# Leaving the residual unscaled: gate and bias divided by alpha, the first residual tiles made in the last merge chunk

## The chip, the cores and the metric

One NeuronCore of a Trainium2 chip runs the whole layer. Its engines are TensorE (PE, and PEld for its weight loads), VectorE (DVE), ScalarE (ACT), GpSimd (POOL) and SyncE (SP); SP and POOL issue nearly all transfers here. The metric is the device time of one execution, in microseconds (us). Engines wait for one another by semaphores written out by hand.

## The reference

One layer of a decoder trunk on `x` of 2048 tokens by 1024 channels, all in float32:

```
h    = x * (1 + scale(c)) + shift(c)
proj = h W_in + b_in                       # q k v | z_attn | u g_b g_c z_conv | two merge gates
y_A  = (dilated attention * silu(z_attn)) W_pA
y_B  = (g_b * conv3(g_c * u) * silu(z_conv)) W_pB
m    = sigmoid(g_A) * y_A + sigmoid(g_B) * y_B
out  = LayerNorm(alpha * x + gate(c) * (m W_out + b_out)) * ln_g + ln_b     # alpha = 2 ** 0.25, eps = 1e-5
```

The mean and variance of the layer norm are taken over the 1024 channels of each token. Where the argument of the norm is divided by alpha, its standard deviation is divided by alpha too; so the same output comes from `x + (gate/alpha) * (m W_out + b_out)`, if the variance is multiplied by alpha squared ahead of eps and the centred value by alpha.

## The kernel before

All products are done in fp32r with each operand split into a high and a low part, in three passes (L1224 high by high, L1229 high by low, L1232 low by high). Big projections are done by a seven-product scheme (`NP = 7`): per group of 2 x 2 blocks, sums and differences of weight blocks are multiplied by sums and differences of activation blocks, and a group's seven results (p0 to p6) are added into four outputs. A product is four matmuls of 128x128 by 128x512 in each of three passes. ScalarE rounds the high parts (`round_w`, `round_t`, `round_to`), VectorE forms the low parts by subtraction (`split_w`, `split_t`, `split_to`) and the sums of weights (`combine`).

The stages, in order: the input projection (`NS` products in all; in it attention, convolution and gates are worked in between; its gate stage forms the `gate` row and multiplies `w_out` by it, one 128-row slice k at a time, `load_wo_raw`, `scale_wo`, `store_wos`); the merge, `NMU = 32` units of 4 token chunks by 8 channel tiles (`project_att`, `project_conv` on TensorE, `gate_att`, `merge` on VectorE, `store_m` on POOL); and the output projection with the norm, 8 groups of seven products, each group two tiles of 128 tokens. `M0 = 24` is the first unit of the last merge chunk. The merged activations take the place of weights in the output projection, and `w_out`'s blocks and their combinations, to(0) to to(6), that of activations; `load_to(p)` on SP waits for the convolution products that last read the places it fills, to(4), to(5) and to(6) for all of them.

The residual. `xs` is a ring of six places for tiles of `x`, 128 tokens by 1024. `load_x(h)` (L907) on SP loads the two tiles of a group, `scale_x` (L1614) on ScalarE multiplies them by alpha, `residual(tt)` (L1159) on POOL adds the row `gb_d` = gate * b_out to all 128 partitions by an accumulating transfer, and `take_y` on VectorE adds the projection's results from PSUM. `take_y(NS)`, the first one, waits for both tiles of its group (`r_in`); it signals `p1_out`, which the third product of the group, p2, waits for, since p0, p2, p4 and p6 of a group share one PSUM bank (`bank`). In the same way p4 waits for `take_y` of p2, and p6 for that of p4.

After that `deviation` (L1606, L1609) on ScalarE and `center` (L2138, L2141) on VectorE finish a tile and `shift_row` (L1163) on POOL stores it. `finish_last` does the last one.

The row gate * b_out is made in the last merge chunk: SP loads `b_out` and `ada_d` (the gate row, stored earlier) as broadcasts (L965, L966), VectorE multiplies them at M0+1 and waits for them there, POOL stores one row to `gb_d` (L1169). The order on each engine is the order of the code: in the last chunk each engine runs its work unit by unit, and in the output projection VectorE's step m takes product m-1, then `center`, `combine`, `split_w(m + 3)` and in the first three steps `split_to`. The stores of the last chunk go to places which the gate loads of units three later reuse (`m_last`); SP issues these loads (L837) in turn with `load_to` (L894).

Of the kernel before, what the change touches and what calls it, by code (L numbers as in the profile page):

```python
# [8 lines left out]
ALU = mybir.AluOpType  # L9
# [190 lines left out]
def build(nc, x, x_t, c, w_ada_t, w_gate, b_ada, cols_h, w_first, w_tiles, w_pa, w_pc, w_out, b_out, ln_g, ln_b, out):  # L200
# [20 lines left out]
    mix_d = dram("mix_d", (KT, P, SEQ))  # L221
    ada_d = dram("ada_d", (1, D))

    with ExitStack() as top:
# [126 lines left out]

        gb = view(3584, D)
        g_bc = view(5632, D)
        b_bc = view(6656, D)
        squares = view(8704, D)
        xs = (view(4608, D), part[:].rearrange("p a n -> p (a n)")[:, 0:D], view(0, D), view(1024, D), view(2048, D), view(7680, D))
        wq = view(3584, 4, CH)
# [106 lines left out]
        gbc_done = sem("gbc_done")  # L464
        ada_out = sem("ada_out")
        wos_ready = sem("wos_ready")
# [32 lines left out]
        gb_ready = sem("gb_ready")  # L499
        x_scaled = sem("x_scaled")  # L500
        r_in = [sem(f"r_in{r}") for r in range(2)]
# [153 lines left out]
        with nc.Block() as block:  # L655
            @block.sync
            def _(sp):
# [48 lines left out]
                def load_t(ph, p):  # L706
                    if p == 0:
                        if ph == 1:
                            for idx in (0, 2, 3):
                                sp.wait_ge(hk_out[idx], 16 * KH)  # L710
                            sp.wait_ge(tk_out, 16 * 4 * KH)
                        if ph == 2:
                            for n in ("b11", "b21", "b22", "t1", "t2", "t3", "rest"):
                                sp.wait_ge(dumped[n], 16)
                            sp.wait_ge(ada_out, 16)
                            sp.wait_ge(za_out, 64)
                            for r in range(2):
                                sp.wait_ge(wos_out[r], 16 * 4)
                    if p >= STAGED:
                        sp.wait_ge(prod, FIRST[ph] - NP + p + 1)  # L720
                    if p >= 4:
                        sp.wait_ge(t_hi_done, NP * ph + T_MORE + p - 3)
                    dst = t_stage[ph][p] if p < STAGED else t_raw[:, p]
                    sp.dma_start(dst, tr_d[(0, 1, 0)[ph], p]).then_inc(t_in[p % 4], 16)
# [39 lines left out]
                def load_wo_raw(k):  # L764
                    sp.wait_ge(gbc_done, 2)
                    if k >= 2:
                        sp.wait_ge(wos_out[k % 2], 16 * (k // 2))
                    sp.dma_start(gate_w[:, k % 2], w_out2[:, k, :]).then_inc(gw_in[k % 2], 16)
# [127 lines left out]
                def load_x(h):  # L896
                    if h == 0:
                        sp.wait_ge(gb_ready, 1)
                    if h in (1, 2):
                        wait_m_last()  # L900
                        sp.wait_ge(ya_done, NMU)
                    if h >= 2:
                        sp.wait_ge(x_scaled, 2 * h - 2)
                    if h >= 3:
                        sp.wait_ge(outs[h % 3], 32 * (h // 3))
                    for tt in (2 * h, 2 * h + 1):
                        sp.dma_start(xs[tt % NX], x2[tt * P:(tt + 1) * P, :]).then_inc(x_in[h % 2], 16)  # L907
# [40 lines left out]
                for n in range(NMU):  # L948
# [10 lines left out]
                    if n == M0:  # L959
                        load_m(0)  # L960
                        load_m(1)
                        load_to(0)
                        sp.wait_ge(ya_done, M0)
                        sp.wait_ge(ada_out, 16)
                        sp.dma_start(gb, b_out.broadcast_to([P, D])).then_inc(bc_in, 16)  # L965
                        sp.dma_start(xs[0], ada_d.broadcast_to([P, D])).then_inc(bc_in, 16)  # L966
                    for p, when in ((1, 3), (2, 4), (3, 6)):
                        if n == M0 + when:
                            load_to(p)
                    if n == M0 + 5:  # L970
                        load_x(0)
                load_to(4)
                load_to(5)
                load_to(6)
                sp.wait_ge(gb_ready, 1)
                sp.wait_ge(ya_done, NMU)
# [17 lines left out]
            def _(pool):  # L994
# [121 lines left out]
                for m in range(NPAIRED, NS + 2):  # L1116
# [21 lines left out]
                    if m - 2 in TWO_AT[1:]:  # L1138
                        store_att(TWO_AT.index(m - 2) - 1)
                    if m == BG2 + 26:  # L1140
                        pool.wait_ge(gbc_done, 2)
                        pool.dma_start(ada_d, gate_bc[0:1, :]).then_inc(ada_out, 16)
                    for k in range(KT):
# [11 lines left out]
                def residual(tt):  # L1155
                    pool.wait_ge(x_scaled, tt + 1)
                    if tt >= 4:
# [7 lines left out]
                for n in range(NMU):  # L1165
                    store_m(n)
                    if n == M0 + 1:
                        pool.wait_ge(gb_ready, 1)
                        pool.dma_start(gb_d, gb[0:1, :]).then_inc(gb_out, 16)  # L1169
                        pool.wait_ge(gb_out, 16)  # L1170
                residual(0)
                residual(1)
                for h in range(NO):
# [242 lines left out]
            def _(act):  # L1416
# [182 lines left out]
                def deviation(tt):  # L1599
                    r = tt % 2  # L1600
                    if tt == LAST:
                        act.wait_ge(var_ready, 1)
                        nc.scalar.activation(std[:, r:r + 1], mv[:, 1:2], ACT.Sqrt, bias=eps[:, 0:1]).then_inc(std_ready, 1)
                        return
# [4 lines left out]
                    nc.scalar.activation(std[:, r:r + 1], ssq[:, r:r + 1], ACT.Sqrt, bias=eps[:, 0:1],  # L1609
                                         scale=1.0 / D).then_inc(std_ready, 1)  # L1610

                def scale_x(tt):
                    act.wait_ge(x_in[tt // 2 % 2], 32 * (tt // 4 + 1))
                    nc.scalar.activation(xs[tt % NX], xs[tt % NX], ACT.Identity, bias=0.0, scale=ALPHA).then_inc(x_scaled, 1)  # L1614

# [70 lines left out]
                for n in range(NMU):  # L1686
# [9 lines left out]
                    for q, when in enumerate((2, 3, 5, 7)):  # L1696
                        if n == M0 + when:
                            round_w(NS + q)
                    if n == M0 + 7:
                        scale_x(0)  # L1700
                        scale_x(1)

                for m in range(NS, NALL + 2):
                    if m + 4 < NALL:
                        round_w(m + 4)
                    if m < NS + 3:
                        round_to(m - NS + 4)
                    h, p = (m - NS) // NP, (m - NS) % NP
                    if p == 3 and h < NO - 1:
                        scale_x(2 * h + 2)  # L1710
                        scale_x(2 * h + 3)
                    if p == 6:
# [5 lines left out]
            def _(dve):  # L1718
# [277 lines left out]
                def scale_wo(k):  # L1996
                    dve.wait_ge(gbc_done, 2)
                    dve.wait_ge(gw_in[k % 2], 16 * ((5, 4)[k % 2] + k // 2 + 1))
                    tt_op(gate_w[:, k % 2], gate_w[:, k % 2], gate_bc, ALU.mult).then_inc(wos_ready, 1)

# [127 lines left out]
                def center(tt):  # L2128
# [5 lines left out]
                    if tt < 2:  # L2134
                        dve.wait_ge(bc_in, 64)
                    dve.wait_ge(nmu_ready, tt + 1)
# [131 lines left out]
                for n in range(NMU):  # L2268
# [10 lines left out]
                    if M0 + 1 <= n <= M0 + 3:  # L2279
                        combine(NG, n - M0 - 1)  # L2280
                    if n == M0 + 1:
                        dve.wait_ge(bc_in, 32)
                        tt_op(gb, gb, xs[0], ALU.mult).then_inc(gb_ready, 1)
                    for p, when in enumerate((2, 5, 6, 7)):
# [66 lines left out]
```

## Time and profile before

| | us |
|---|---|
| median of 3 runs | 1878.07 (1877.03 to 1879.09) |
| the profiled execution | 1877.03 |
| its span in the trace | 1875.2 |
| TensorE busy | 1831.5 (98%) |
| VectorE busy | 1241.3 (66%) |
| ScalarE busy | 876.3 (47%) |
| GpSimd busy | 201.6 (11%) |

The profiled execution is one of the three runs; its span is 1.8 us shorter than its time. In the timeline a row is: start, duration, engine, line, operation, written tile and read tiles, shapes, count, and in brackets the idle time of the engine ahead of it with what ended it. A row of windows is: the stretch; its length, then for each engine (PE, PEld, DVE, ACT, POOL) busy time and count of instructions; then the granted TensorE clock (1.00 is full), the share in which the 16 DMA engines moved data, and GB/s. `room` is the large scratch area in SBUF; many tiles lie in it, some of the `xs` among them; `part` is another such place. A row for SPq or POOL with DMA_DIRECT2D is the issue of a transfer.

### The profile page before, as it was taken

The numbers are of one execution on the slowest core, as the hardware profiler recorded it, in microseconds if no ns is written. First come the engines' busy times: TensorE is split into PE (matmuls) and PEld (weight loads), VectorE is DVE, ScalarE is ACT, GpSimd is POOL, SyncE is SP. The second block draws the span as 40 slices with busy tenths as digits, with TensorE's granted clock in tenths as the row PEclk, the third lists the DMA queues.
The fourth block names the chain that finished last, engine by engine and source line by source line (L and its number), as shares of the span: only waits on it lengthen the run. The fifth ranks groups of instructions, "written<-read, shape, count | busy, mean of one in ns | idle before, by whom it ended". The sixth has DMA issues, their size and how long they took to land.

```text
span 1875.2 us, 24771 instructions
## 1 busy us (share of the span) xinstructions
PE 1831.5 (98%) x8783; PEld 1490.9 (80%) x8783; DVE 1241.3 (66%) x2185; ACT 876.3 (47%) x1567; POOL 201.6 (11%) x327
## 2 busy tenths in 40 slices
PE   8999999999999999999999999999999999996997
PEld 7788888888888888877878888888888888885875
DVE  8755744456666666665686666666577665646886
ACT  5544633445555555666665445545444400014442
POOL 0223011100000000111110000000111000001110
PEclk9999999999999999999999999999999999998998
DMA  9866523332222222555762222232583987777782
GB/s 371 297 231 242 201 108 112 104 120 85 97 97 85 85 95 82 177 178 194 275 225 93 79 90 80 85 107 85 177 291 120 346 219 198 234 255 220 211 227 86
DMA packets 162234, 312.32 MB, mean 167 GB/s; under 512 B 35808, under 2 KB 87776, under 8 KB 157888
## 3 DMA queue, kind: packets, MB, share of 16 engines
q1 hardware_dynamic: 133072, 209.68, 34.5%
q0 software_dynamic: 28752, 100.46, 15.8%
q8 instruction: 71, 1.16, 0.3%
q10 hardware_dynamic: 288, 0.59, 0.1%
q14 instruction: 51, 0.42, 0.1%
HBM read 218.10 MB, written 92.58 MB: 166 GB/s over the span
## 4 chain that ended last, share of the span: by engine, by line
PE 86%; DVE 5%; DMA 4%; issue 2%; ACT 1%; SPq 1%; POOL 0%; DVEq 0%; ACTq 0%
PE acc L1224 23%; PE acc L1229 23%; PE acc L1232 23%; PE acc L1378 2%; PE acc L1386 2%; PE acc L1382 2%; PE score L1289 2%; PE xb L1322 2%; DVE room L1725 1%; DVE t_lo L1725 1%; PE acc L1240 1%; PE xb L1305 1%; PE pt_o L1305 1%; DMA part<-gb_d 1%; DMA vt_d<-room 1%
## 5 line engine op out<-in xcount | busy, mean ns | idle before, releaser
L1224 PE MATMUL acc<-t_hi,w_hi 128*128 128x512 f32 x1888 | 519.7, 397 | 5.5 <-DVE room L1725 4.4
L1229 PE MATMUL acc<-t_lo,w_hi 128*128 128x512 f32 x1888 | 505.8, 390 | 0.0
L1232 PE MATMUL acc<-t_hi,w_lo 128*128 128x512 f32 x1888 | 505.4, 389 | 0.0
L1229 PEld LDWEIGHTS acc<-t_lo,w_hi 128*128 128x128 f32 x1888 | 354.4, 188 | 75.8
L1232 PEld LDWEIGHTS acc<-t_hi,w_lo 128*128 128x128 f32 x1888 | 354.4, 188 | 74.9
L1224 PEld LDWEIGHTS acc<-t_hi,w_hi 128*128 128x128 f32 x1888 | 344.5, 188 | 86.7 <-issue 13.7
L1725 DVE TENSOR_TENSOR room<-acc,part 128x512 f32<-128x512 f32 x198 | 136.7, 690 | 216.6 <-PE acc L1232 214.8
L1505 ACT ACTIVATE part<-acc,cols 128x512 f32<-128x512 f32 x198 | 136.5, 689 | 209.3 <-PE acc L1232 208.9
L1725 DVE TENSOR_TENSOR w_lo<-w_raw,w_hi 128x512 fp32r<-128x512 f32 x278 | 187.4, 686 | 38.7 <-ACT w_hi L1488 37.1
L1488 ACT CAST w_hi<-w_raw 128x512 fp32r<-128x512 f32 x270 | 166.2, 616 | 99.0 <-PE acc L1232 96.7
L1488 ACT CAST w_hi<-s_tmp 128x512 fp32r<-128x512 f32 x203 | 125.6, 619 | 177.9 <-PE acc L1232 146.7
L1725 DVE TENSOR_TENSOR room<-room 128x512 f32<-128x512 f32 (+3 forms) x217 | 156.3, 724 | 62.7 <-ACT room L1535 30.6
L1725 DVE TENSOR_TENSOR w_lo<-s_tmp,w_hi 128x512 fp32r<-128x512 f32 x203 | 139.4, 687 | 64.7 <-ACT w_hi L1488 62.3
L1570 ACT ACTIVATE room<-room 128x128 f32<-128x128 f32 (+1 forms) x192 | 86.4, 451 | 54.8 <-DVE room L1971 54.6
L1076 POOL DMA_DIRECT2D att_d<-room x48 | 34.5, 718 | 529.9 <-DVE room L1978 529.9
L1725 DVE TENSOR_TENSOR w_raw<-w_raw 128x512 f32<-128x512 f32 x98 | 67.4, 688 | 5.0 <-DVE room L1725 0.5
L1967 DVE CUSTOM_DVE_ANT_0 room<-score,room 128x128 f32<-128x128 f32 (+1 forms) x192 | 58.7, 362 | 17.1 <-PE score L1289 16.8
L1725 DVE TENSOR_TENSOR s_tmp<-w_raw,s_tmp 128x512 f32<-128x512 f32 x74 | 51.0, 690 | 27.5 <-PE acc L1232 24.4
L1725 DVE TENSOR_TENSOR t_lo<-t_raw,t_hi 128x2048 fp32r<-128x2048 f32 (+1 forms) x29 | 57.6, 1992 | 14.4 <-ACT t_hi L1597 10.7
L1589 ACT CAST t_hi<-t_raw 128x2048 fp32r<-128x2048 f32 x6 | 11.4, 1907 | 113.5 <-DMA t_raw<-conv_d 113.5
L1098 POOL DMA_DIRECT2D gate_d<-room x64 | 34.9, 547 | 243.2 <-ACT room L1521 243.1
L1224 PE MATMUL acc<-t_hi 128*128 128x512 f32 x152 | 42.1, 399 | 17.7 <-DVE room L1725 17.7
(257 smaller groups left out, 2102.1 us busy)
## 6 DMA issues: line engine op xcount, KB each, us to landing
w_raw<-in_w_tiles SPq DMA_DIRECT2D x132, 512.0 KB, 4.4
gate_d<-room POOLq DMA_DIRECT2D x64, 256.0 KB, 3.9
qk_d<-room POOLq DMA_DIRECT2D x24, 512.0 KB, 5.1
w_raw<-gate_d SPq DMA_DIRECT2D x24, 512.0 KB, 6.2
room<-qk_d SPq DMA_DIRECT2D x74, 128.0 KB, 3.1
t_raw<-tr_d SPq DMA_DIRECT2D x8, 1024.0 KB, 7.2
conv_d<-room POOLq DMA_DIRECT2D x16, 512.0 KB, 3.0
w_raw<-mix_d SPq DMA_DIRECT2D x16, 512.0 KB, 7.3
```

The source lines that it names most:

```text
L1224: nc.tensor.matmul(to, hi_w[:, k], hi_t[:, k], start=(first and k == 0), stop=False, skip_group_check=True)
L1229: nc.tensor.matmul(to, hi_w[:, k], lo_t[:, k], start=False, stop=False, skip_group_check=True)
L1232: mm = nc.tensor.matmul(to, lo_w[:, k], hi_t[:, k], start=False, stop=(last and k == KH - 1), skip_group_check=True)
L1289: mm = nc.tensor.matmul(sc_ps[:, h, columns(j, s)], q_two[rows_h, s], keys, start=True, stop=True)
L1305: tr = nc.tensor.transpose((po, xb)[s][:, (2 * h + half) * P:(2 * h + half + 1) * P], prob[:, h, (2 * s + half) * P:(2 * s + half + 1) * P ...
L1322: mm = nc.tensor.matmul(o_ps[cols_h, s * P:(s + 1) * P], v_two[:, s + half, cols_h], prob_t[:, s, (2 * h + half) * P:(2 * h + half + 1) * ...
L1378: nc.tensor.matmul(to, w_h[:, k], b_half(True, k), start=(k == 0), stop=False)
L1488: nc.scalar.copy(w_slot(hi_parts, n), src).then_inc(hi_done, 1)
L1505: ins = nc.scalar.activation(to, src, ACT.Identity, bias=col(gr.tb if p == 1 else gr.ta))
L1570: ex = nc.scalar.activation(prob[:, h, o], prob[:, h, o], ACT.Exp, bias=all_m[:, t, h, b], scale=SCALE, accum_out=all_d[:, t, h, b])
L1725: return nc.vector.tensor_tensor(o, a, b, op)
L1967: own_t.up(nc.vector.tensor_tensor_reduce(out=prob[:, h, o], in0=sc_ps[:, h, o], in1=bm[:, h, o.start - 2 * P * s:2 * P], scale=1.0, scala ...
```

## The change

- `x` is no longer scaled. `scale_wo` multiplies `w_out` by gate and by 1/alpha, the bias row is gate * b_out / alpha, `deviation` uses alpha squared, and `g_bc` (ln_g on all partitions) is multiplied by alpha once, on ScalarE in step NS+4.
- The bias row is formed in the gate stage, on one partition, just ahead of the first `scale_wo`, and POOL stores it to `gb_d` there. `ada_d` and the two broadcasts in the last merge chunk are gone.
- `load_x(0)` goes from unit M0+5 to M0+2; `residual(0)` and `residual(1)` go from behind the merge loop to behind `store_m(M0 + 3)` in POOL's queue.
- The ring of `xs` has other places, so that `load_x(1)` and `load_x(2)` no longer wait for the last merge stores.
- `residual(tt)` waits for the load of `x` itself.

```diff
-        xs = (view(4608, D), part[...][:, 0:D], view(0, D), view(1024, D), view(2048, D), view(7680, D))
+        xs = (part[...][:, 0:D], view(4608, D), view(3584, D), view(7680, D), view(9728, D), view(10752, D))
@@ SP
                 def load_wo_raw(k):
                     sp.wait_ge(gbc_done, 2)
+                    if k == 0:
+                        sp.dma_start(gate_acc[0:1], b_out).then_inc(b_row_in, 16)
...
                 def load_x(h):
                     if h == 0:
-                        sp.wait_ge(gb_ready, 1)
+                        sp.wait_ge(ya_done, M0)
                     if h in (1, 2):
-                        wait_m_last()
                         sp.wait_ge(ya_done, NMU)
                     if h >= 2:
-                        sp.wait_ge(x_scaled, 2 * h - 2)
+                        sp.wait_ge(r_in[h % 2], 32 * (h // 2))
...
                     if n == M0:
                         load_m(0)
                         load_m(1)
                         load_to(0)
-                        sp.wait_ge(ya_done, M0)
-                        sp.wait_ge(ada_out, 16)
-                        sp.dma_start(gb, b_out.broadcast_to([P, D])).then_inc(bc_in, 16)
-                        sp.dma_start(xs[0], ada_d.broadcast_to([P, D])).then_inc(bc_in, 16)
...
-                    if n == M0 + 5:
+                    if n == M0 + 2:
                         load_x(0)
...
-                sp.wait_ge(gb_ready, 1)
@@ POOL
-                    if m == BG2 + 26:
-                        pool.wait_ge(gbc_done, 2)
-                        pool.dma_start(ada_d, gate_bc[0:1, :]).then_inc(ada_out, 16)
+                    if m == BG2 + 29:
+                        pool.wait_ge(gb_ready, 1)
+                        pool.dma_start(gb_d, gate_acc[0:1]).then_inc(gb_out, 16)
...
                 def residual(tt):
-                    pool.wait_ge(x_scaled, tt + 1)
+                    pool.wait_ge(x_in[tt // 2 % 2], 32 * (tt // 4 + 1))
...
                 for n in range(NMU):
                     store_m(n)
-                    if n == M0 + 1:
-                        pool.wait_ge(gb_ready, 1)
-                        pool.dma_start(gb_d, gb[0:1, :]).then_inc(gb_out, 16)
+                    if n == M0 + 3:
                         pool.wait_ge(gb_out, 16)
-                residual(0)
-                residual(1)
+                        residual(0)
+                        residual(1)
@@ ScalarE
-                def scale_x(tt):
-                    act.wait_ge(x_in[tt // 2 % 2], 32 * (tt // 4 + 1))
-                    nc.scalar.activation(xs[tt % NX], xs[tt % NX], ACT.Identity, bias=0.0, scale=ALPHA).then_inc(x_scaled, 1)
...
+                    if m == NS + 4:
+                        act.wait_ge(bc_in, 32)
+                        nc.scalar.activation(g_bc, g_bc, ACT.Identity, bias=0.0, scale=ALPHA).then_inc(g_scaled, 1)
...
-                    if p == 3 and h < NO - 1:
-                        scale_x(2 * h + 2)
-                        scale_x(2 * h + 3)
@@ VectorE
                 def scale_wo(k):
                     dve.wait_ge(gbc_done, 2)
+                    if k == 0:
+                        dve.wait_ge(b_row_in, 16)
+                        nc.vector.scalar_tensor_tensor(out=gate_acc[0:1], in0=gate_acc[0:1], scalar=1.0 / ALPHA, in1=gate_bc[0:1],
+                                                       op0=ALU.mult, op1=ALU.mult).then_inc(gb_ready, 1)
                     dve.wait_ge(gw_in[k % 2], 16 * ((5, 4)[k % 2] + k // 2 + 1))
-                    tt_op(gate_w[:, k % 2], gate_w[:, k % 2], gate_bc, ALU.mult).then_inc(wos_ready, 1)
+                    nc.vector.scalar_tensor_tensor(out=gate_w[:, k % 2], in0=gate_w[:, k % 2], scalar=1.0 / ALPHA, in1=gate_bc,
+                                                   op0=ALU.mult, op1=ALU.mult).then_inc(wos_ready, 1)
...
-                    if n == M0 + 1:
-                        dve.wait_ge(bc_in, 32)
-                        tt_op(gb, gb, xs[0], ALU.mult).then_inc(gb_ready, 1)
```

## Rows read from the trace of the kernel before

**Rows 1.** The page's head: the span and its instructions.

```profile
span 1875.2 us, 24771 instructions
```

**Rows 2.** TensorE's waits over the span: total, times, longest.

```profile
PE acc L1224 <- DVE room L1725: 22.0, 12, 15.9
```

**Rows 3.** Windows over the start of the output projection.

```profile
1686.20:1691.80 5.60, 5.60 (x25) 4.32 (x23) 3.86 (x4) 5.20 (x6) 0.00 (x0) 1.00 0.85 292
1691.80:1707.70 15.90, 0.01 (x1) 0.00 (x0) 2.43 (x6) 6.14 (x5) 2.39 (x3) 0.57 1.04 330
1707.70:1723.00 15.30, 15.27 (x60) 12.31 (x61) 15.14 (x21) 5.02 (x7) 1.71 (x2) 0.89 0.63 148
```

**Rows 4.** The chain of waits from 1686 to 1732: start, duration, what.

```profile
1693.54 13.27 DMA part<-gb_d
```

**Rows 5.** Timeline, 1664 to 1708.

```profile
1672.26 0.47 SPq L907 DMA_DIRECT2D room<-in_x  x1
...
1673.34 0.57 SPq L894 DMA_DIRECT2D t_raw<-wos_d  x1
...
1685.96 1.91 ACT L1597 CAST t_hi<-t_raw 128x2048 fp32r<-128x2048 f32 x1 [4.64 <-DMA t_raw<-wos_d]
1686.21 1.07 PE L1224 MATMUL acc<-t_hi 128*128 128x512 f32 x4
...
1687.90 2.29 DVE L1725 TENSOR_TENSOR t_lo<-t_raw,t_hi 128x2048 fp32r<-128x2048 f32 x1 [2.85 <-ACT t_hi L1597]
...
1691.21 1.90 ACT L1597 CAST t_hi<-t_raw 128x2048 fp32r<-128x2048 f32 x1 [0.40 <-DMA t_raw<-to_d]
1691.43 0.69 DVE L1725 TENSOR_TENSOR room<-room 128x512 f32<-128x512 f32 x1
...
1693.90 1.90 ACT L1597 CAST t_hi<-t_raw 128x2048 fp32r<-128x2048 f32 x1 [0.27 <-DMA t_raw<-wos_d]
...
1696.43 1.90 ACT L1597 CAST w_hi<-wl_raw 128x2048 fp32r<-128x2048 f32 x1
```

**Rows 6.** Timeline, 1707 to 1731: p2, p3, p4 and p6, then the next group.

```profile
1707.73 2.05 PE L1224 MATMUL acc<-t_hi 128*128 128x512 f32 x4 [15.92 <-DVE room L1725]
...
1712.13 1.07 PE L1224 MATMUL acc<-t_hi 128*128 128x512 f32 x4
...
1714.85 1.07 PE L1224 MATMUL acc<-t_hi,w_hi 128*128 128x512 f32 x4
...
1720.36 1.17 PE L1224 MATMUL acc<-w_hi,t_hi 128*128 128x512 f32 x4
...
1723.21 1.07 PE L1224 MATMUL acc<-t_hi 128*128 128x512 f32 x4
...
1730.13 1.17 PE L1224 MATMUL acc<-t_hi,w_hi 128*128 128x512 f32 x4 [1.32 <-DVE room L1725]
```

**Rows 7.** Timeline of the last merge chunk: its first matmul; VectorE's wait at M0+1.

```profile
1631.81 0.39 PE L1356 MATMUL score<-o_hi_b,pa_hi 128*128 128x512 f32 x1
...
1652.29 1.23 DVE L1725 TENSOR_TENSOR room<-room 128x1024 f32<-128x1024 f32 x1 [9.78 <-DMA room<-ada_d]
```

**Rows 8.** Landing times: merge stores 1630 to 1700; then L907; then L1159.

```profile
DMA to landing us min/median/max: 2.3/5.3/7.8
...
DMA to landing us min/median/max: 8.2/9.4/11.1
...
DMA to landing us min/median/max: 4.9/8.0/13.3
```

**Rows 9.** Window of ten microseconds in and behind the hole.

```profile
1690.00:1700.00 10.00, 1.81 (x9) 1.16 (x7) 3.39 (x7) 7.54 (x7) 2.39 (x3) 0.70 1.02 360
```

**Rows 10.** Timeline, gate stage: the first `scale_wo`, and VectorE's next longer idle time.

```profile
864.90 1.22 DVE L1725 TENSOR_TENSOR room<-room 128x1024 f32<-128x1024 f32 x1
...
871.93 0.42 DVE L1978 COPY room<-xb 128x256 f32<-128x256 f32 x1 [4.59 <-PE xb L1322]
```

**Rows 11.** Groups of instructions, 1631 to 1876: the scaling of `x`.

```profile
L1614 ACT ACTIVATE room<-room 128x1024 f32<-128x1024 f32 x13 | 13.2, 1052 | 0.0
```

More of the change, by code:

```diff
@@ L221, in build @@
     mix_d = dram("mix_d", (KT, P, SEQ))
-    ada_d = dram("ada_d", (1, D))
     with ExitStack() as top:
@@ L350, in build @@
         mst = w_flat[:, 6 * CH:8 * CH].rearrange("p (a n) -> p a n", a=2)
-        gb = view(3584, D)
         g_bc = view(5632, D)
@@ L355, in build @@
         squares = view(8704, D)
-        xs = (view(4608, D), part[:].rearrange("p a n -> p (a n)")[:, 0:D], view(0, D), view(1024, D), view(2048, D), view(7680, D))
+        xs = (part[:].rearrange("p a n -> p (a n)")[:, 0:D], view(4608, D), view(3584, D), view(7680, D), view(9728, D), view(10752, D))
         wq = view(3584, 4, CH)
@@ L464, in build @@
         gbc_done = sem("gbc_done")
-        ada_out = sem("ada_out")
+        b_row_in = sem("b_row_in")
+        g_scaled = sem("g_scaled")
         wos_ready = sem("wos_ready")
@@ L499, in build @@
         gb_ready = sem("gb_ready")
-        x_scaled = sem("x_scaled")
         r_in = [sem(f"r_in{r}") for r in range(2)]
@@ L714, in load_t @@
                                 sp.wait_ge(dumped[n], 16)
-                            sp.wait_ge(ada_out, 16)
+                            sp.wait_ge(gb_out, 16)
                             sp.wait_ge(za_out, 64)
@@ L962, in _ @@
                         load_to(0)
-                        sp.wait_ge(ya_done, M0)
-                        sp.wait_ge(ada_out, 16)
-                        sp.dma_start(gb, b_out.broadcast_to([P, D])).then_inc(bc_in, 16)
-                        sp.dma_start(xs[0], ada_d.broadcast_to([P, D])).then_inc(bc_in, 16)
                     for p, when in ((1, 3), (2, 4), (3, 6)):
@@ L1602, in deviation @@
                         act.wait_ge(var_ready, 1)
-                        nc.scalar.activation(std[:, r:r + 1], mv[:, 1:2], ACT.Sqrt, bias=eps[:, 0:1]).then_inc(std_ready, 1)
+                        nc.scalar.activation(std[:, r:r + 1], mv[:, 1:2], ACT.Sqrt, bias=eps[:, 0:1],
+                                             scale=ALPHA ** 2).then_inc(std_ready, 1)
                         return
@@ L1609, in deviation @@
                     nc.scalar.activation(std[:, r:r + 1], ssq[:, r:r + 1], ACT.Sqrt, bias=eps[:, 0:1],
-                                         scale=1.0 / D).then_inc(std_ready, 1)
-                def scale_x(tt):
-                    act.wait_ge(x_in[tt // 2 % 2], 32 * (tt // 4 + 1))
-                    nc.scalar.activation(xs[tt % NX], xs[tt % NX], ACT.Identity, bias=0.0, scale=ALPHA).then_inc(x_scaled, 1)
+                                         scale=ALPHA ** 2 / D).then_inc(std_ready, 1)
                 for d in range(KT):
@@ L1698, in _ @@
                             round_w(NS + q)
-                    if n == M0 + 7:
-                        scale_x(0)
-                        scale_x(1)
                 for m in range(NS, NALL + 2):
@@ L2134, in center @@
                     if tt < 2:
-                        dve.wait_ge(bc_in, 64)
+                        dve.wait_ge(g_scaled, 1)
                     dve.wait_ge(nmu_ready, tt + 1)
```

## The prediction

> **What bounds the kernel now.** I read the page's head, the tensor engine's waits, the windows over the last stages, the chain of waits and then the timeline around the one long hole. The span is 1875.2 us [rows 1]. TensorE waits 22.0 us in all for VectorE's `room` writes at L1725, and 15.9 of them in one piece [rows 2]. The windows put that piece between 1691.8 and 1707.7: no matmul but one in 15.9 us, the DMA engines full (share 1.04), the granted clock 0.57; in the window after it TensorE is busy throughout, at 0.89 [rows 3]. The chain names what ended the hole: the landing of the accumulating transfer `part<-gb_d`, issued at 1693.54, 13.27 us later [rows 4]. That is `residual(1)`, and `take_y(NS)`, the first result of the output projection, waits for the pair `residual(0)`, `residual(1)`. POOL issues the pair after its last merge store, since `residual` stands behind the loop. I number the projection's seven products of a group p0 to p6. p0 starts at 1686.21 and a product takes 2.72 (p4's first matmul, 1714.85, less p3's, 1712.13), so p1 ends at 1691.65; p2 writes p0's bank, must wait for `take_y(NS)`, and starts at 1707.73 [rows 5, 6]. Nothing else of that size is left in the last stages.
>
> **The first pair of residual tiles.** With `x` unscaled, the pair needs only x(0) and `gb_d`. `gb_d` is then written in the gate stage, some 750 us earlier. The merge chunk starts at 1631.81 and its eight units end with 1686.21, 6.80 us each, with no hole [rows 5, 7]. Unit M0+1 ends at 1645.4, its merge is two 0.69 us operations (1646.8), its store lands 5.3 us later (median), so SP passes the gate load of M0+4 and issues x(0) near 1653. x(0) lands within 8.2 to 11.1 us [rows 8], by 1664. POOL reaches M0+3 at 1659.0 + 1.4 + 0.5 = 1661, waits for x(0) up to 3 us, and issues both tiles by 1665. Residuals have taken 4.9 to 13.3 us to land: they are there between 1670 and 1679. They are wanted at 1689, when p0 ends at 1688.93. So this wait goes, with 10 us to spare.
>
> **What is late next.** VectorE. Its queue ahead of `take_y(NS)` holds split_to(3), which waits for ScalarE's cast of to(3): loaded at 1673.34, cast at 1685.96 on landing, split at 1687.90, and the last merge ended at 1691.43 + 0.69 [rows 5]. x(0)'s 1 MB was issued just ahead of that load; at the 360 GB/s of this stretch [rows 9] 1 MB is 2.9 us, so to(3) now lands near 1683.0. Then the cast 1.9, split_to(3) 2.29, one weight split 0.69, merge 1.38, a combine and a split 1.38, take_y(NS) 0.69: 1691.3, just ahead of p1's end at 1691.65. p2 starts with no stall and p3 ends at 1697.1. p4 shares the bank with p2 and waits for `take_y(NS+2)`, which is behind split_to(4) and split_to(5) in the queue. to(4) and to(5) are issued when the last convolution product is done, unchanged, and their casts end at 1691.21 + 1.90 = 1693.1 and 1693.90 + 1.90 = 1695.8 [rows 5]. VectorE: 1693.1, split_to(4) 2.29, take p1 and a split 1.38, split_to(5) 2.29, take p2 0.69, that is 1699.8. New stall 2.7 us. p4 ends at 1702.5, p5 at 1705.2. VectorE goes on with 1.38, split_to(6) 2.29, take p3, two small ones and take p4 (four of 0.69): 1706.2, which p6 waits for (1.0 us). p6 takes 2.85 after such a wait (1720.36 to 1723.21), and p0 of the next group starts at 1709.0; before it started at 1723.21 [rows 6]. From there to p2 of that group it took 6.92 (1730.13) and will again, since `center` follows the end of p6 as before. Gain 14.2 us.
>
> In this figure are 16.1 us of hole gone, 1.7 us of slow clock gone (p2 took 1712.13 less 1707.73, that is 4.40 in place of 2.72, after the hole), and 3.7 us of new, short waits.
>
> **The rest, at nothing.** Sixteen scale operations on ScalarE of 1.05 us [rows 11] go, fourteen of them in the projection, where TensorE's short wait at a group's border is for VectorE; cover is not needed. One 1.06 us operation is added, scaling `g_bc`, behind the landing of ln_g and ln_b. ScalarE may be held at it until some 1703; the next cast behind it waits for p4's end at 1702.5 anyway and is wanted by VectorE only near 1709: nothing, and if the landing is 5 us later than that, still nothing. `scalar_tensor_tensor` takes the place of a multiply for the eight slices of `w_out`, and there is one row of 1024 more in the gate stage: the multiply took 1.22 at 864.90 and VectorE then idled 4.59 us before 871.93 [rows 10]; the trace of before has neither at this place, so I bound each between nothing and twice that multiply, 2.4, and take 1.22, since all have 1024 elements a partition. At 2.4 both together add 3.6 to this step, under the 4.59: covered at either end, and without the cover the eight slices and the row would be 1 to 11 us. The b_out row's 4 KB load is ahead of a 512 KB one that the same step waits for: nothing. In the merge chunk VectorE loses its 9.78 us wait for `room<-ada_d` and the 1.23 multiply [rows 7]; TensorE had no hole there, so this earns nothing itself, but two 512 KB broadcasts go out of SP's queue. POOL's `gb_d` store moves ahead of store_wos(0), whose producer is the next instruction on VectorE: nothing.
>
> Sum against the profiled execution's own 1877.03: 1862.8. The median of the runs is 1.04 above that execution; I forecast 1863.9.
>
> **Rivals.** (A) The second pair becomes the wait. x(1) and x(2) are now issued near 1689, behind to(4), to(5), to(6), ln_g and ln_b. From to(6)'s cast at 1696.43, 1 MB of ln_g and ln_b and 1 MB of x(1) at 360 GB/s end at 1702.2; residual(2) and (3) are issued by 1704, beside x(2) and the next 1 MB of merged rows, and are wanted near 1714.5 (p2 of group 1 less 0.8). Median landing 8.0 gives 1712, in time; 13.3 gives 1717, 2.7 late, and if x(1) itself lands at its 11.1 behind ln_b, 5. Time 1866.7 to 1869. Against: half the range of landings is on the early side. The Trainium skill (DMA: Bandwidth & Descriptors, Queues, rings and completion order) says that a completion count lands only after every earlier write of that DMA engine, of all its queues; then residual(3) is not done before the x(2) writes ahead of it, near 1705 at the rate above, which gives the same time but raises this rival's chance. No row of before tells it apart, since the slow residual of rows 4 had x(1) and x(2) behind it, not ahead. 0.20.
> (B) to(3) lands no sooner. The residuals now stand ahead of the store of unit M0+4 in POOL's queue, and SP's gate load of M0+7, ahead of to(3), waits for that store. If to(3) lands at 1685.9 as before, take_y(NS) ends at 1694.2 and p2 to p4 shift by 2.5, the stalls behind shrink, and 12.7 is gained (1865.4); each microsecond beyond costs one, to 1870 for 4.6. 0.12.
> (C) Slower: B to its end. Store of M0+1 at 7.8, x(0) at 11.1, the pair at 13.3, the store of M0+4 at 7.8 behind it and to(3) at 12.6, all largest values: 1646.8 + 0.5 + 7.8 + 1 + 11.1 + 0.9 + 13.3 + 7.8 + 1 + 12.6 = 1702.8, p2 starts 8.3 later, at 1711.1, 3.4 us later than now: about 1881.5. It decides where to(3) lands after 1699.4. Against: the DMA share over this chunk leaves room, and the 13.3 was in a full stretch. 0.04.
> (D) The change doesn't do it: something else holds take_y(NS), and under 3.8 us is gained: 1875 to 1878. 0.03.
> (E) to(4) and to(5) land sooner and part of the 3.7 goes too: 1860.5 to 1863. With no wait left from p1 to p2 of the next group, that p2 starts at 1691.65 + 7 x 2.72 = 1710.7, 19.4 earlier: the limit is 1858.7. 0.08.
>
> **Chances.** Forecast 0.53 with its own range of 1862.8 to 1866. About 0.2% (3.8 us) is what a measurement of this kernel can tell from no change. Faster by more: forecast, A, B, E, 0.93; within: 0.03; slower: 0.04. The range is 1861.0 to 1869.5: it leaves out the far end of E, the end of B, C and D.
>
> **What will show it.** The hole at 1691.8 gone and the clock at full level through it; x(0) and both first residuals issued before 1666; p2 directly behind p1; a wait of 2 to 3 us before p4 and about 1 before p6, released by L1725; the span from p2 of group 1 to the end unchanged at 145.1; the merge chunk free of holes. Wrong if a DMA releases `take_y(NS)` or `take_y(NS+7)`, if the merge chunk's units grow over 6.80, or if a group of the projection takes over 19.7.

## The result, and the profile after

| | before | after |
|---|---|---|
| median of 5 runs, us | 1878.07 (1876.77 to 1880.03) | 1862.71 (1861.51 to 1869.59) |
| ratio, 95% | 1 | 0.9927 (0.9907 to 0.9946) |
| the same kernels once more | 1877.79 (15 runs) | 1862.0 (4 runs), 0.9918 (0.9904 to 0.9931) |
| and again | 1877.95 (9 runs) | 1862.26 (5 runs), 0.992 (0.9908 to 0.9933) |

The forecast was 1863.9, a gain of 14.2 us; the gain is 15.4 of the medians, then 15.8 and 15.7.

The execution profiled first is the slowest of its five, 1869.59. It is 7.6 us behind before when the output projection starts, at p0, and all of that lies ahead of the last merge chunk, where no wait grew. Three rows of it show the largest piece, at a reload of `w_out`'s slices that stands at the same place in both kernels: VectorE waits for a DMA in the convolution product, then TensorE for VectorE, and then TensorE's clock stands at half (1.2 GHz) for 6.8 us.

```profile
1364.88 2.87 DVE L1711 TENSOR_TENSOR room<-room 128x512 f32<-128x512 f32 x4 [6.46 <-DMA room<-wos_d]
1375.29 2.04 PE L1216 MATMUL acc<-t_hi,w_hi 128*128 128x512 f32 x4 [2.96 <-DVE room L1711]
```

```profile
1374.50:1381.30 6.80, 6.01 (x14) 4.79 (x15) 5.46 (x10) 3.56 (x6) 1.86 (x3) 0.50 0.76 293
```

Two further profiled executions of the same kernel reach p0 at 1686.03 and 1684.91, before at 1686.21: the piece at 1375 is in neither. So I read executions by stage, each against its own p0, and show the one of 1862.45 us. Its head, then TensorE's waits (which answer to [rows 2]), then the window of the old hole (to [rows 3]):

```profile
span 1860.6 us, 24749 instructions
```

```profile
PE acc L1216 <- DVE room L1711: 4.9, 9, 1.3
...
PE acc L1216 <- ACT t_hi L1480: 3.0, 1, 3.0
```

```profile
1686.00:1691.60 5.60, 5.60 (x26) 4.63 (x25) 5.01 (x9) 0.56 (x1) 0.54 (x1) 1.00 0.70 252
1691.60:1707.50 15.90, 12.82 (x56) 10.01 (x55) 13.98 (x18) 9.54 (x10) 1.78 (x2) 1.00 1.03 383
```

The piece of 15.9 us is gone from the waits; the longest one left on a VectorE row is 1.3. In the window TensorE works 12.82 us of 15.90 in place of 0.01, at full clock, beside DMA engines as full as before (1.03). The timeline of the same execution answers to [rows 5] and [rows 6]: first the issue of the pair on POOL and of the loads on SP, then to(3) and p0 to p6, then p2 of the next group.

```profile
1652.06 0.47 SPq L906 DMA_DIRECT2D part<-in_x  x1
...
1661.27 0.93 POOL L1153 DMA_DIRECT2D part<-gb_d  x1
1661.85 1.25 POOL L1153 DMA_DIRECT2D room<-gb_d  x1
...
1674.37 0.47 SPq L894 DMA_DIRECT2D t_raw<-wos_d  x1
...
1682.37 1.91 ACT L1589 CAST t_hi<-t_raw 128x2048 fp32r<-128x2048 f32 x1 [2.09 <-DMA t_raw<-wos_d]
...
1686.03 1.07 PE L1216 MATMUL acc<-t_hi 128*128 128x512 f32 x4
...
1689.81 0.68 DVE L1711 TENSOR_TENSOR part<-acc,part 128x512 f32<-128x512 f32 x1
...
1691.47 1.07 PE L1216 MATMUL acc<-t_hi 128*128 128x512 f32 x4
...
1699.22 0.68 DVE L1711 TENSOR_TENSOR part<-acc,part 128x512 f32<-128x512 f32 x1
...
1700.05 1.17 PE L1216 MATMUL acc<-t_hi,w_hi 128*128 128x512 f32 x4 [2.98 <-ACT t_hi L1480]
...
1702.90 1.78 POOL L1153 DMA_DIRECT2D room<-gb_d  x2 [13.53 <-DMA room<-in_x]
...
1705.88 1.17 PE L1216 MATMUL acc<-w_hi,t_hi 128*128 128x512 f32 x4
...
1708.71 1.07 PE L1216 MATMUL acc<-t_hi 128*128 128x512 f32 x4
...
1715.64 1.16 PE L1216 MATMUL acc<-t_hi,w_hi 128*128 128x512 f32 x4 [1.32 <-DVE room L1711]
```

p2 (1691.47) follows p1 with no wait, since `take_y(NS)` at 1689.81 waits for no DMA. The one wait of size left is ahead of p4. Its bracket names a ScalarE cast; take_y(NS+2) at 1699.22 ended within 0.02 us of it. In the other two executions of the same kernel the bracket of p4 names two other rows:

```profile
1707.18 1.16 PE L1216 MATMUL acc<-t_hi,w_hi 128*128 128x512 f32 x4 [2.36 <-DVE part L1711]
```

```profile
1698.34 1.17 PE L1216 MATMUL acc<-t_hi,w_hi 128*128 128x512 f32 x4 [2.39 <-ACT w_hi L1589]
```

An experiment below (takes_first) tells which of them counts.

For all kernels below, starts of products after p0's, read from each trace (q0 and q2 are p0 and p2 of the next group; the last column is from q2 to the end):

```
                   p2     p4     p6     q0     q2    to end
before           21.52  28.64  34.15  36.99  43.91  145.06
after, first      5.44  13.40  19.23  22.05  29.00  144.97
after, second     5.44  14.02  19.85  22.69  29.61  144.92
after, third      5.44  13.43  20.61  23.33  29.60  144.88
pair_late        19.77  27.35  32.79  35.51  42.16  144.89
scaled_early      7.85  14.65  20.47  23.30  30.94  145.00
x_late            5.44  13.38  20.54  23.26  30.30  144.86
before_x_behind  20.37  27.48  33.00  35.82  42.76  144.96
pair_m6           5.44  15.64  23.89  26.61  32.87  144.97
x0_at5            9.60  17.51  23.09  25.93  32.85  144.97
takes_first       5.44  11.22  18.05  20.89  29.01  146.57
takes_and_table   5.44  11.31  18.13  20.97  29.54  147.73
early_table       5.44  13.41  20.58  23.30  29.29  144.94
broadcasts_back   8.00  15.28  21.11  23.93  30.87  144.97
```

In this stage the change gains 43.91 less 29.61, that is 14.3 us in the second and third execution, 14.9 in the first; behind q2 at most 0.2.

### The profile page after: what moved, and what is told of

It is laid out like the page before. It is cut to its first block, busy times and chain, and to the rows that moved or that the text cites. A ratio compares the mean times of both kernels' runs of the same rounds, so it can differ in the third digit from the quotient of the medians.

```text
span 1867.8 us, 24749 instructions
## 1 busy us (share of the span) xinstructions
PE 1833.3 (98%) x8783; PEld 1491.7 (80%) x8783; DVE 1242.3 (67%) x2185; ACT 862.1 (46%) x1552; POOL 200.7 (11%) x326
## 3 DMA queue, kind: packets, MB, share of 16 engines
q0 software_dynamic: 28720, 100.46, 15.9%
## 4 chain that ended last, share of the span: by engine, by line
PE 89%; DVE 4%; DMA 2%; issue 2%; ACT 1%; SPq 1%; POOL 0%; DVEq 0%; ACTq 0%
PE acc L1216 23%; PE acc L1221 22%; PE acc L1224 22%; PE acc L1370 3%; PE acc L1378 3%; PE acc L1374 3%; PE score L1281 2%; PE xb L1314 2%; PE acc L1232 1%; PE xb L1297 1%; DVE room L1711 1%; PE pt_o L1297 1%; DVE t_lo L1711 1%; DMA vt_d<-room 1%; SPq L783 1%
## 5 line engine op out<-in xcount | busy, mean ns | idle before, releaser
L1711 DVE TENSOR_TENSOR room<-room 128x512 f32<-128x512 f32 (+2 forms) x208 | 145.4, 703 | 48.5 <-ACT room L1527 30.6
L1711 DVE TENSOR_TENSOR t_lo<-t_raw,t_hi 128x2048 fp32r<-128x2048 f32 (+1 forms) x29 | 57.6, 1994 | 15.7 <-ACT t_hi L1589 12.1
L1581 ACT CAST t_hi<-t_raw 128x2048 fp32r<-128x2048 f32 x6 | 11.4, 1908 | 113.4 <-DMA t_raw<-conv_d 113.4
L1711 DVE TENSOR_TENSOR s_tmp<-w_raw 128x512 f32<-128x512 f32 x74 | 51.0, 690 | 5.4 <-DMA w_raw<-mix_d 0.9
```

The source lines that it names most:

```text
L1711: return nc.vector.tensor_tensor(o, a, b, op)
```

## The experiments

Two of the runs were the changed kernel again, without an edit, for the rows and medians above.

> The changed kernel once more, unaltered. Its profiled execution of 1869.59 us was 7.6 us behind the kernel before when the last merge chunk began, in three pieces (0.9 at 20 us, 1.3 at 74 us, 5.3 between 1365 and 1382 us, where VectorE waited for a reload of w_out's slices and the clock then fell for 6.8 us), and 14.9 us ahead of that offset after the hole. Theory: those early pieces are chance of single executions, not the change; then this run has a median of 1861.5 to 1864 and an execution without them. Rival: the early pieces belong to the change (its gate stage); then they are in every execution and the median of several new rounds is 1865 or more.

> The changed kernel unaltered, beside the next three on the same chip: 1861 to 1863.5, p2 of group 1 at 29.6 us behind p0 of group 0.

Measured: 1862.0 and 1862.26.

**pair_late: the pair back behind the merge loop, all else of the change kept.**

```diff
                         pool.wait_ge(gb_out, 16)
-                        residual(0)
-                        residual(1)
+                residual(0)
+                residual(1)
```

> The changed kernel with residual(0) and residual(1) put back behind the merge loop in POOL's queue, all else as changed. Theory (the place of the pair is the gain): they are issued near 1693 on the old time scale, land 9 to 14 us later among to(5), to(6), ln_g, ln_b and x(1), the hole behind p1 is back with 11 to 16 us and the time is 1873 to 1879. Rival (the unscaled x and the two broadcasts less are the gain): the time stays at 1863 to 1866.

Measured: 1874.69 (11 runs), 0.9985 of before (0.9976 to 0.9993). The hole is back, and the same transfer ends it: POOL's issue, VectorE's take and TensorE's p2.

```profile
1689.86 0.93 POOL L1153 DMA_DIRECT2D part<-gb_d  x1
1690.43 1.25 POOL L1153 DMA_DIRECT2D room<-gb_d  x1
...
1704.78 0.69 DVE L1711 TENSOR_TENSOR part<-acc,part 128x512 f32<-128x512 f32 x1 [14.40 <-DMA room<-gb_d]
```

```profile
PE acc L1216 <- DVE part L1711: 14.2, 1, 14.2
```

The place of the two `residual` calls is worth 12.7 us of the medians, 12.55 at q2 (42.16 less 29.61). All other edits together are left with 3.1 of the medians, 1.75 in this stage, and no run moves the pair alone in the kernel before. In pair_late the pair is issued 4.0 and 4.6 us behind p0 (1685.84), in before 6.7 and 7.3.

**scaled_early: `x` scaled on ScalarE again, the pair at M0+4.**

```diff
                 def residual(tt):
-                    pool.wait_ge(x_in[tt // 2 % 2], 32 * (tt // 4 + 1))
+                    pool.wait_ge(x_scaled, tt + 1)
...
-                    if n == M0 + 3:
+                    if n == M0 + 4:
                         pool.wait_ge(gb_out, 16)
...
+                    if n == M0 + 3:
+                        scale_x(0)
+                        scale_x(1)
...
+                    if p == (3 if h else 5) and h < NO - 1:
+                        scale_x(2 * h + 2)
+                        scale_x(2 * h + 3)
```

(All factors of alpha elsewhere are 1 in it.)

> The changed kernel with x scaled on ScalarE again (all factors 1/alpha and alpha squared set to 1): the first two tiles at unit M0+3, their residuals behind the store of M0+4, the other tiles at step 5 of the first group and step 3 of the later ones. Theory: ScalarE has room, so 1862.5 to 1866, within 2 us of the changed kernel. Rival (unscaled x is itself worth much): the scale operations hold ScalarE's casts or the second pair of tiles, 1868 or more.

Measured: 1866.39 (1865.7 to 1867.96), 3.7 to 4.4 above the changed kernel's three medians. It lies between my range and the rival's, 0.4 over the top of mine. Of this 1.3 is in the stage at q2. to(3) lands behind the later pair, so p2 starts 2.4 later and the wait before p4 shrinks. The second pair then waits for ScalarE's scaling, and `take_y(NS+7)` for the pair, 0.62 us, a small case of rival A's wait. POOL's issue of it:

```profile
1709.06 1.82 POOL L1154 DMA_DIRECT2D room<-gb_d  x2 [14.45 <-ACT room L1608]
```

So an unscaled `x` is no condition of most of the gain: with the scaling kept, 11.4 us came, of 15.8. About 2 us of this kernel's distance lie ahead of p0 in its profiled execution, which is what equal kernels differ by there.

**x_late: x(1) and x(2) wait again for the last merge stores.**

```diff
                     if h in (1, 2):
+                        wait_m_last()
                         sp.wait_ge(ya_done, NMU)
```

> The changed kernel with the loads x(1) and x(2) again held until all stores of the last merge chunk have landed (the new ring makes this needless). Theory A: they are issued 7 to 10 us later, residual(2) and residual(3) land 2 to 6 us after they are wanted and p2 of group 1 waits for them: 1865 to 1869. Theory B (there is slack): no wait of that kind, 1861.5 to 1864.

Measured: 1864.04 (1863.04 to 1868.58), 0.9934 (0.992 to 0.9947); q2 is 0.7 later. x(1) is issued 7.6 us later than in the changed kernel, and `take_y(NS+7)` now waits for the second pair:

```profile
1715.65 0.69 DVE L1712 TENSOR_TENSOR room<-acc,room 128x512 f32<-128x512 f32 x1 [0.69 <-DMA room<-gb_d]
```

Theory A's wait is there, smaller than its 2 to 6 us, and the time is B's, at the very top of its range. The new places of the `xs` ring are mostly slack; the intervals of this kernel and the changed one overlap.

**before_x_behind: the kernel before, with x(1) and x(2) held until the first residual pair has landed.**

```diff
                     if h in (1, 2):
+                        sp.wait_ge(r_in[0], 32)
                         wait_m_last()
```

> The kernel before, with the loads x(1) and x(2) held until both first residual tiles have landed. Theory (the 13.3 us landing was the pair sharing the DMA engines with 2 MB of x behind it and ln_g, ln_b ahead): the pair lands in 7 to 10 us, the hole of 15.9 us shrinks by 3 to 6, the second pair comes later but before it is wanted at 1729: 1872 to 1875.5. Rival (an accumulating transfer of this size is slow by itself): landing still 12 us or more, 1877 to 1879.

Measured: 1876.88 (11 runs), 0.9992 (0.9982 to 1.0002), not told from no change; time and landing fall between the theory's ranges and the rival's. The pair still takes 9.6 to 11.4 us to land in place of 10.1 to 13.3, is issued 0.7 later, and p2 starts 1.2 sooner. The first row is VectorE's wait in this kernel, the others are the landing times of this pair here, of the pair in pair_late, and of the pair in pair_m6 (next):

```profile
DVE room L1726 <- DMA part<-gb_d: 11.6, 1, 11.6
```

```profile
DMA to landing us min/median/max: 9.6/10.5/11.4
```

```profile
DMA to landing us min/median/max: 11.0/12.6/14.3
```

```profile
DMA to landing us min/median/max: 5.1/6.1/7.2
```

So the 2 MB of `x` behind the pair made at most 1.9 of its 13.3 us. to(5), to(6), ln_g and ln_b stay ahead of or beside it here, and it stays slow; that it is they was not tried alone.

**pair_m6 and x0_at5: the pair at M0+6; in the second, x(0) back at M0+5 too.**

```diff
-                    if n == M0 + 3:
+                    if n == M0 + 6:
                         pool.wait_ge(gb_out, 16)
...  in x0_at5 also
-                    if n == M0 + 2:
+                    if n == M0 + 5:
                         load_x(0)
```

> The changed kernel with the first pair behind the store of unit M0+6 in place of M0+3; x(0) still loaded at M0+2. Theory: POOL issues it at 1681 to 1685, it lands 7 to 11 us later, at 1689 to 1695, and it is wanted at 1689.8: p2 waits 0 to 4 us, 1862 to 1866. Between the changed kernel (1862.0) and the pair behind the loop (1874.7), and nearer to the first, since to(4), to(5) are late anyway. Rival (any place inside the loop is as good): 1861.5 to 1863.

> The changed kernel with x(0) loaded at M0+5 as before, and so its pair behind the store of M0+6. Theory: x(0) is again issued just ahead of to(3); to(3) lands near 1685.5 instead of 1682.4, the pair is issued near 1684 and lands near 1693: take_y of p0 waits 2 to 5 us, 1864 to 1867. Rival (the load's place is worth nothing): the same time as with x(0) at M0+2 and the pair at M0+6.

Measured: 1867.22 (0.9942, 0.9929 to 0.9954) and 1866.67 (0.9937, 0.9924 to 0.9951). pair_m6 misses my 1866 by 1.2, and not by the wait that I had named. The take waits 0.56 us for its pair, p2 still follows p1 with no wait. But to(4), issued at the same distance from p0, now has the pair in flight beside it and lands 7.0 us after its issue in place of 4.8; its cast stands 7.25 behind p0 in place of 5.01, that of to(5) 10.54 in place of 9.03. p4 comes at 15.64 and the clock stands at half, so that p4 to p5 takes 5.26 in place of 2.84. In x0_at5 the take waits 2.38 us for the pair, and TensorE 4.0 at p2. First the take and to(4)'s cast in pair_m6, then its window, then VectorE's wait in x0_at5:

```profile
1691.06 0.69 DVE L1711 TENSOR_TENSOR part<-acc,part 128x512 f32<-128x512 f32 x1 [0.56 <-DMA room<-gb_d]
...
1694.78 1.91 ACT L1589 CAST t_hi<-t_raw 128x2048 fp32r<-128x2048 f32 x1 [9.43 <-DMA t_raw<-to_d]
```

```profile
1702.10:1708.90 6.80, 5.74 (x14) 4.51 (x15) 6.37 (x10) 2.66 (x5) 1.72 (x2) 0.50 1.02 368
```

```profile
1696.25 0.69 DVE L1711 TENSOR_TENSOR part<-acc,part 128x512 f32<-128x512 f32 x1 [2.38 <-DMA room<-gb_d]
```

Both reach q2 at 32.9. The pair three units later costs 3.3 us there, and x(0)'s place nothing beyond that: one wait at p2 took the place of one before p4. to(3) does feel x(0)'s place: its cast stands 5.12 ahead of p0 in pair_m6 and 1.13 in x0_at5, since SP issues it 3.0 later and it lands 1.0 slower.

**takes_first: `take_y(NS+2)` ahead of split_to(5) and `take_y(NS+4)` a step sooner in VectorE's queue; early_table: the square root table loaded once ahead of the merge chunk; takes_and_table: both.**

```diff
 takes_first (VectorE)
-                    if m > NS:
+                    if m > NS and m not in (NS + 3, NS + 5):
                         take_y(m - 1)
+                    if m == NS + 4:
+                        take_y(NS + 4)
...
+                    if m == NS + 2:
+                        take_y(NS + 2)
                     if NS < m <= NS + 3:
                         split_to(m - NS + 3)
 early_table (ScalarE)
+                    if n == M0:
+                        act.wait_ge(sig_c, 3)
+                        nc.scalar.activation(c_e[:, 0:1], c_e[:, 0:1], ACT.Sqrt, bias=0.0)
```

> The changed kernel with VectorE's order changed at the projection's start: the takes of p2 and p4 ahead of split_to(5) and ahead of the combine and weight split behind split_to(6). Theory (the new waits before p4 and p6 are VectorE's queue): p4 starts near 1697.2 in place of 1700.05, p6 near 1704.7 in place of 1705.9, so 1.2 us less: 1860.8. Rival (the wait is for the landing of to(4) and to(5), order does nothing): 1862.0.

> The changed kernel with one Sqrt of one column on ScalarE at unit M0, so that the table load of 1.28 us ahead of the first deviation is done there. Theory: center of group 0 no longer waits 0.84 us for ScalarE, and p2 of group 1 starts 0.8 us sooner, at 28.8: 1861.2 where the changed kernel has 1862.0. Rival: VectorE's queue is the bound there and nothing changes.

> Both: VectorE takes p2 and p4 first, and the table load is early. With the first alone p6 started 1.8 us sooner but p2 of group 1 only 0.6, since center waited 1.39 us for ScalarE behind that load. Theory: with both, p2 of group 1 starts at 27.8 to 28.2 and the time is 1.4 to 1.8 us under the changed kernel's: 1860.4. Rival: the border's wait grows again by what is saved, and nothing is left.

Measured: 1864.9 (0.9931, 0.9919 to 0.9944), 1863.03 (0.992, 0.9907 to 0.9934), 1865.75 (0.9936, 0.9923 to 0.9948): none beats the changed kernel, and all three forecasts of a gain (1860.8, 1861.2, 1860.4) are missed. In takes_first p4 starts 2.8 us sooner than in the second execution of the change and 2.2 sooner than in the others, at 11.22, with a wait of 0.18. Only VectorE's order was changed, so the wait before p4 was VectorE's; the cast that the bracket had named ends 13.9 behind p0 in the second execution and 13.7 here, behind p4's start. p6 and q0 keep 1.8 of it against the second execution, q2 only 0.6, and against the first, whose q2 is at 29.00, nothing. Of takes_first: the table load on ScalarE that `center` now waits for, and TensorE's wait at q2.

```profile
1709.99 1.28 ACT L1602 ACT_TABLE_LOAD   x1
...
1711.62 0.16 DVE L2124 RECIPROCAL rstd<-std 128x1 f32<-128x1 f32 x1 [1.39 <-ACT std L1602]
...
1716.47 1.15 PE L1216 MATMUL acc<-t_hi,w_hi 128*128 128x512 f32 x4 [2.52 <-DVE room L1711]
```

```profile
1717.60:1721.00 3.40, 3.40 (x10) 2.62 (x9) 3.30 (x6) 0.00 (x0) 1.34 (x3) 0.50 0.14 54
```

With that table load out of the way too, in takes_and_table, VectorE's take ahead of q2 waits for the second residual pair:

```profile
1716.35 0.69 DVE L1714 TENSOR_TENSOR room<-acc,room 128x512 f32<-128x512 f32 x1 [1.63 <-DMA room<-gb_d]
```

That is rival A's wait, 1.6 us long, once TensorE comes 1.7 us sooner. The two kernels pay 1.6 and 2.8 us more behind q2, where the clock stood at half for 3.4 and 6.8 us. early_table has no wait for the table load left, but its q2 (29.29) lies among those of the changed kernel (29.00 to 29.61): no gain shows.

**broadcasts_back: two 512 KB broadcasts in SP's queue ahead of x(0), and x(0) waiting for them, as before.**

```diff
                         load_to(0)
+                        sp.wait_ge(ya_done, M0)
+                        sp.dma_start(view(3584, D), b_out.broadcast_to([P, D])).then_inc(extra_in, 16)
+                        sp.dma_start(xs[1], b_out.broadcast_to([P, D])).then_inc(extra_in, 16)
...
                     if h == 0:
                         sp.wait_ge(ya_done, M0)
+                        sp.wait_ge(extra_in, 32)
```

> The changed kernel with two 512 KB broadcast loads of b_out put back at M0 in SP's queue, to places that nothing reads; x(0) waits for both. Theory: their traffic is early in the chunk and costs nothing, x(0) lands 3 us later at most: 1861 to 1864. Rival (2 to 3 us of the gain came from the broadcasts being gone): 1864 to 1866.

Measured: 1864.93 (1862.85 to 1869.08), 0.9933 (0.992 to 0.9946), in the rival's range. to(3)'s cast and the wait in p2 in this kernel:

```profile
1691.14 1.91 ACT L1594 CAST t_hi<-t_raw 128x2048 fp32r<-128x2048 f32 x1 [3.63 <-DMA t_raw<-wos_d]
...
1699.40 1.19 PE L1221 MATMUL acc<-t_hi 128*128 128x512 f32 x2 [2.40 <-DVE part L1716]
```

p0 starts at 1691.40 here, so to(3) lands 0.26 us ahead of it; in the changed kernel 3.66 ahead, in before 0.25 [rows 5]. SP issues it 8.65 ahead of p0, the changed kernel 11.66 (1674.37 against 1686.03). The two broadcasts and the wait for them cost p2 2.6 us and q2 1.3 in this one execution, the slowest of its five, whose p0 is 5.4 us late from ahead of the last merge chunk. The medians differ by 2.7, with intervals that overlap.

## Why the prediction was right

The forecast's steps, each by the second execution of the change, whose p0 is 0.18 before that of the kernel before:

- **What bounds it.** The hole and its releaser: confirmed by pair_late, which brings both back at 12.7 us.
- **The first pair.** x(0) was to be issued near 1653 and was at 1652.06 and 1652.57; the pair by 1665, and was at 1661.27 and 1661.85, then landed 9.0 to 11.1 us later, so by 1673, where 1670 to 1679 was forecast. It is needed at 1688.75. x(0) itself landed in 5.3 to 6.0 us, under the 8.2 to 11.1 that I took. In this stretch the DMA engines were full too (0.99 from 1660 to 1673), but nobody waited.
- **p2.** to(3) at 1683.0, measured 1682.37. take_y(NS) was to end at 1691.3 and ended at 1690.5; p2 without a stall, as forecast.
- **p4.** 1699.8 against 1700.05, its wait 2.7 against 2.98. to(5)'s cast came 1.2 later than taken, of which VectorE waited 0.53. takes_first shows that the reason given, split_to(5) ahead of the take, is the right one.
- **p6, q0, q2.** 1706.2, 1709.0 and 1715.9 against 1705.88, 1708.71 and 1715.64. The wait before p6 was to be 1.0 and was 0.3 (0.5 in the third execution).
- **The sum.** 14.2 against 14.3 in the stage, and 14.9 in the first execution; that it fits to 0.1 is luck, since equal kernels differ by 0.6 at q2 and single terms are off by up to 0.7. The hole and its slow clock gave 17.8, the new wait and a small one take some 3.5. The second execution gains 14.6 over its whole span, and its time, 1862.45, is 14.58 under 1877.03. The medians gain 1.2 to 1.6 more than 14.2, which is within what single executions of one kernel differ by ahead of p0; no row accounts for it. With this excess the three medians (1862.71, 1862.0, 1862.26) lie 0.1 to 0.8 under the forecast's own 1862.8 to 1866, inside rival E's 1860.5 to 1863, though E's cause did not occur.

**What was off.** The median of 5.3 us for merge stores [rows 8] counts four loads of the same tensor in; the nine stores alone have 3.4. x(0)'s time came out right all the same, by luck. The second pair was put as wanted near 1714.5, but 1715.9 less 0.8 is 1715.1; the take started at 1714.81. The larger miss is what it said of the two broadcasts taken out of SP's queue, "this earns nothing itself". The forecast explained to(3)'s earlier landing by x(0) gone from in front of it, 2.9 us. The landing did shorten, from 12.6 us to 8.0 after the issue, but broadcasts_back, where x(0) is also out of the way and to(3) lands in 8.4, has it at 0.26 before p0, as before: SP is 3.0 us later there, and that eats it all. In x0_at5 the broadcasts are gone and x(0) is late, and to(3) gains only 0.9. So both edits were needed for the 3.4 us that to(3) gained, and the reason given for it, 1 MB less in front, is shown only in part: between pair_m6 and x0_at5, which differ in x(0)'s place alone, 1.0 us of 4.0 is in the landing and 3.0 in SP's issue. The sum was right because the two edits were made together. Also off is the size of scaling: ScalarE's scale operations at nothing holds for TensorE's short waits at a group's border, but scaled_early has the second pair wait behind one (1.3 us at q2, of which part is to(3)).

**The gate stage.** The row of 1024 took 1.21 us and each slice 1.22, the value taken between nothing and 2.4; VectorE's idle time went from 4.59 [rows 10] to 4.09, still covered. VectorE's rows of the second execution:

```profile
865.27 1.21 DVE L1986 SCALAR_TENSOR_TENSOR room<-room 1x1024 f32<-1x1024 f32 x1
866.41 1.21 DVE L1989 SCALAR_TENSOR_TENSOR room<-room 128x1024 f32<-128x1024 f32 x1
872.30 0.42 DVE L1964 COPY room<-xb 128x256 f32<-128x256 f32 x1 [4.09 <-PE xb L1314]
```

**The rivals.** A (second pair): in time in the change. x(1) releases it at 1702.90 (forecast: by 1704; the four loads of `x` took 12.5 to 14.8 us, over the range that I had), it lands 8.2 to 10.9 us later, just ahead of need; x_late, scaled_early and takes_and_table make VectorE's take wait for it (0.6 to 1.6 us), so A was near, within 1 us of deciding. The Trainium skill (DMA: Bandwidth & Descriptors, Queues, rings and completion order) says that a completion count lands only after every earlier write of that DMA engine, of all its queues. The pair did complete after x(1) and x(2), whose slowest load took 14.8 us from its issue, but it was issued behind them in any case, so this does not test the rule. B (to(3) no sooner) did not occur; broadcasts_back shows what it would have cost at q2, 1.3 us, near the 1.5 given for it. Its cause is there at a small size: in pair_m6, where the pair is not ahead of the store of M0+4, SP issues to(3) 13.4 ahead of p0, in the changed kernel 11.4 to 11.7. C and D did not occur: the stores and gate loads of the chunk held no unit, p0 is 54.4 us, eight units of 6.80, behind the chunk's start. E: to(4) and to(5) were not sooner, 5.0 and 9.0 us behind p0 at their casts, before 5.0 and 7.7.

## What to carry to other kernels

A transfer that the first take of a new stage waits for belongs in the queue of the stage before, where its source is ready; look for its inputs' true producers. Here the multiply by a constant seemed to tie it to a late stage, but scaled_early keeps it and most of the gain: what tied the transfer was the place of its call. A transfer moved up can also be moved next to others that matter: at M0+6 it slowed to(4) and cost 3.3 us, at M0+3 nothing waited for it. Once a large hole is filled, work out the next wait on each engine in turn before hoping for more: here VectorE's queue, a table load and the second pair stood within 1 to 3 us of each other, and none of three attempts on them was measurably faster. Judge steps of a few microseconds by the distances within the stage in several executions, because a single one can be 7 us off before the stage begins.

## What the runs showed beside this

TensorE's granted clock after short waits was not the same from one execution to the next. Behind a wait before p4 of 2.98 us in the second execution of the change, and of 2.36 in the first, it stayed at full level (2.4 GHz). In the third, with 2.39, and in x_late and early_table it stood at half for 3.4 us near 1700, in pair_m6 for 6.8 us from 1702.1. From p4 to p6 the third took 7.2 us in place of 5.8, and yet it reaches q2 at the same distance, since p4 had come 0.6 sooner and p6 to q2 took 9.0 in place of 9.8. Why the clock falls behind one such wait and not behind another, the runs don't tell.

Landing times of the same 512 KB accumulating transfer went from 5.1 us (pair_m6, DMA share 0.86 from 1683 to 1690) to 14.3 (pair_late), with the range of before 4.9 to 13.3 [rows 8]: at one size, the time went with the place of issue. A full DMA share alone doesn't give it: at a share of 0.99 the first pair landed in 9.0 to 11.1 us.
